# Modulation vectors by a product and a row sum on VectorE, instead of column products and matmuls on ones

## The reference

```
c_act = jax.nn.silu(c)                                 # c: (1, 1024)
for i in range(2):
    mod = c_act @ ada_w[i] + ada_b[i]                  # ada_w[i]: 1024 x 6144
    shift_t, scale_t, gate_t, shift_c, scale_c, gate_c = split(mod, 6)
    h = rmsnorm(x, norm_g[i, 0]) * (1.0 + scale_t) + shift_t
    x = x + gate_t * mixer(h)
    h = rmsnorm(x, norm_g[i, 1]) * (1.0 + scale_c) + shift_c
    x = x + gate_c * (square(relu(h @ mlp_w1[i])) @ mlp_w2[i])
```

## Time and profile before

| | us |
|---|---|
| median of 3 runs (1731.29 to 1733.81) | 1731.69 |
| the profiled execution | 1736.6 |
| its span, first to last instruction | 1735.3 |

### The profile page before, as it was taken

One profiled execution on the slowest core, in us unless ns is written; L12 is line 12 of the kernel. 1 busy time (PEld: TensorE's weight loads), 2 busy tenths in 40 slices (PEclk: granted clock), 3 DMA queues, 4 the chain that ended last, 5 costly groups with the idle time before them and its releaser, 6 DMA issues.

```text
span 1735.3 us, 18334 instructions
## 1 busy us (share of the span) xinstructions
PE 1609.7 (93%) x7266; PEld 1267.5 (73%) x7266; DVE 974.5 (56%) x1444; ACT 685.3 (39%) x1120; POOL 208.4 (12%) x194
## 2 busy tenths in 40 slices
PE   1899999799999999999998989999999899999877
PEld 1578877578888887676665768888888776777665
DVE  6665655655667564554445344343434549987544
ACT  3343432532323133444444353232323345455543
POOL 2000001100000001200000110000000103565401
PEclk9999999899999999999999989999999999999989
DMA  6534443445555533111111124333222122112111
GB/s 227 214 120 134 132 135 97 145 136 189 188 177 191 189 103 99 62 49 49 61 49 37 62 79 133 97 97 97 98 96 93 62 88 69 60 44 73 37 49 48
DMA packets 52133, 180.80 MB, mean 104 GB/s; under 512 B 5728, under 2 KB 6624, under 8 KB 51920
## 3 DMA queue, kind: packets, MB, share of 16 engines
q1 hardware_dynamic: 52048, 179.64, 31.7%
HBM read 176.08 MB, written 3.41 MB: 103 GB/s over the span
## 4 chain that ended last, share of the span: by engine, by line
PE 82%; DVE 7%; ACT 6%; POOL 2%; DMA 2%; issue 1%; SPq 0%; DVEq 0%; ACTq 0%; POOLq 0%
PE PS L424 23%; PE PS L427 22%; PE PS L425 22%; PE PS L616 2%; DVE sb_ADA L1377 2%; DVE sb_Wl L1361 1%; PE PS L438 1%; PE PS L445 1%; PE PS L627 1%; PE PS L643 1%; PE PS L740 1%; POOL sb_TMD L1970 1%; DMA sb_ARW<-ada 1%; ACT sb_Wh L896 1%; PE PS L653 1%
## 5 line engine op out<-in xcount | busy, mean ns | idle before, releaser
L424 PE MATMUL PS<-sb_Hh,sb_Wh 128*128 128x512 f32 (+2 forms) x1144 | 471.1, 412 | 21.5 <-DVE sb_Hl L1410 16.8
L427 PE MATMUL PS<-sb_Hh,sb_Wl 128*128 128x512 f32 (+2 forms) x1144 | 454.9, 398 | 0.5 <-DVE sb_Wl L1361 0.5
L425 PE MATMUL PS<-sb_Hl,sb_Wh 128*128 128x512 f32 (+2 forms) x1144 | 454.5, 397 | 0.0
L1361 DVE TENSOR_TENSOR sb_Wl<-sb_RAW,sb_Wh 128x1024 fp32r<-128x1024 f32 (+1 forms) x231 | 296.7, 1286 | 138.8 <-ACT sb_Wh L896 138.3
L896 ACT ACTIVATE sb_Wh<-sb_RAW 128x1024 fp32r<-128x1024 f32 (+1 forms) x231 | 241.8, 1048 | 248.2 <-PE PS L427 227.5
L424 PE MATMUL PS<-sb_Oh,sb_Wh 128*128 128x512 f32 x704 | 279.6, 397 | 2.8 <-DVE sb_Ol L1427 2.3
L424 PEld LDWEIGHTS PS<-sb_Hh,sb_Wh 128*128 128x128 f32 (+2 forms) x1144 | 219.7, 192 | 81.3 <-issue 30.6
L425 PE MATMUL PS<-sb_Ol,sb_Wh 128*128 128x512 f32 x704 | 276.0, 392 | 0.0
L427 PE MATMUL PS<-sb_Oh,sb_Wl 128*128 128x512 f32 x704 | 276.0, 392 | 0.0
L425 PEld LDWEIGHTS PS<-sb_Hl,sb_Wh 128*128 128x128 f32 (+2 forms) x1144 | 219.7, 192 | 50.2 <-issue 5.1
L427 PEld LDWEIGHTS PS<-sb_Hh,sb_Wl 128*128 128x128 f32 (+2 forms) x1144 | 218.9, 191 | 50.6 <-issue 1.0
(11 more groups left out here) (301 smaller groups left out, 1619.8 us busy)
## 6 DMA issues: line engine op xcount, KB each, us to landing
sb_RAW<-w SPq DMA_DIRECT2D x128, 512.0 KB, 3.5
sb_ARW<-ada SPq DMA_DIRECT2D x96, 512.0 KB, 4.5
sb_RAW<-gla_in SPq DMA_DIRECT2D x24, 512.0 KB, 3.6
sb_RAW<-diff_in SPq DMA_DIRECT2D x24, 512.0 KB, 3.5
sb_RAW<-in_b SPq DMA_DIRECT2D x16, 512.0 KB, 3.7
sb_RAW<-gla_wo SPq DMA_DIRECT2D x8, 512.0 KB, 3.6
sb_RAW<-diff_wo SPq DMA_DIRECT2D x8, 512.0 KB, 3.5
sb_RAW<-wo SPq DMA_DIRECT2D x8, 512.0 KB, 3.5
```

Of the source, the lines that this page charges most:

```text
L424: mm(to[0:m, :], Wh[:, si, k, 0:m], hi[:, k, :], start=first, stop=False)
L425: mm(to[0:m, :], Wh[:, si, k, 0:m], lo[:, k, :], start=False, stop=False)
L427: ins = mm(to[0:m, :], Wl[:, si, k, 0:m], hi[:, k, :], start=False, stop=last)
L1361: tt(Wl[:, b % 3, :, 0:m], RAW[:, b % 3, 0:8 * m].rearrange("p (k m) -> p k m", k=8), Wh[:, b % 3, :, 0:m].bitcast(F), ALU.subtract).then_ ...
```

## The change

The weights of the modulation are laid out transposed on the host: a transfer now brings 128 outputs, one on each partition, with all 1024 inputs along the row, again 512 KB. c is put on all partitions, and silu is computed there at full width, by exp, an addition, ln, exp and a product. For each transfer VectorE does one `tensor_tensor_reduce` of 128x1024: product with `CB`, row sum that begins at the bias, result in one column of `MOD`. For a scale column one small operation of one column follows. `ada_sum`, `ada_tick` and `modulation` go, with the 24 groups. Readers wait for single columns. In the start the order is by pairs of scale and shift columns for part j of h, and the weights of blocks 0, 1 and 2 are issued after transfers 3, 5 and 7. The slots of transfers 16 to 95 stay.

```diff
-ADA_GROUPS = [(0, 2), (0, 0), (0, 3), (0, 1)] + [(G // 12, G % 12) for G in range(4, 24)]
-ADA_SUM = {b + 1: s // 4 for b, s in ADA_AT.items() if s % 4 == 3}
+ADA_TILES = [(0, 8 * a + j) for j in range(8) for a in (1, 0)] + [(t // 48, t % 48) for t in range(16, 96)]
...
             def ada(s):
-                layer, g = ADA_GROUPS[s // 4]
                 if s >= 3:
-                    e.wait_ge(at("ada", s - 3, 1))
-                e.op.dma_start(ARW[:, s % 3, :], D["ada"][layer, g, s % 4]).then_inc(*landed(f"ada{s % 3}", s))
+                    e.wait_ge(at("mod", *ADA_TILES[s - 3]))
+                e.op.dma_start(ARW[:, s % 3, :], D["ada"][ADA_TILES[s]]).then_inc(*landed(f"ada{s % 3}", s))
...
             e.op.dma_start(vec[:], D["vec"]).then_inc(*landed("vec"))
+            e.op.dma_start(CB[:], D["c"].to_broadcast([P, 1024])).then_inc(*landed("c"))
...
-            for s in range(8):
+            for s in range(16):
                 ada(s)
-            weights(0)
-            weights(1)
-            for s in range(8, 16):
-                ada(s)
-            weights(2)
+                if s in (3, 5, 7):
+                    weights((s - 3) // 2)
...
-            e.wait_ge(at("ada_pe", 23))
+            e.wait_ge(at("mod", 1, 47))
...
-            def ada_sum(G):
-                to, free = TB.take(("ada", G), ("mod",) + ADA_GROUPS[G])
-                e.wait_ge(at("ada", 4 * G + 3, 1), at("one"), *free)
-                for c in range(4):
-                    ins = mm(to[:, c:c + 1], ADA[:, G % 2, c * 128:(c + 1) * 128], ones[:, 0:1], start=True, stop=True)
-                ins.then_inc(*done("ada_pe", G))
...
-            ada_sum(0)
             stat(0)
-            ada_sum(1)
-            ada_sum(2)
...
-            act(ctmp[:, 0:8], V("c", 0, 8), ACT.Exp, scale=-1.0).then_inc(*done("c_exp"))
+            cs = TMD[:].rearrange("p a t -> p (a t)")
+            e.wait_ge(at("c"))
+            act(cs, CB[:], ACT.Exp, scale=-1.0).then_inc(*done("c_exp"))
+            e.wait_ge(at("c_one"))
+            act(cs, cs, ACT.Ln).then_inc(*done("c_ln"))
+            e.wait_ge(at("c_ln"))
+            act(cs, cs, ACT.Exp, scale=-1.0).then_inc(*done("c_inv"))
...
             def ada(s):
-                G, part = s // 4, s % 4
-                acc = ADA[:, G % 2, :]
+                layer, t = ADA_TILES[s]
+                w, col = ARW[:, s % 3, :], MOD[:, layer, t:t + 1]
                 e.wait_ge(at(f"ada{s % 3}", s), at("cact"))
-                for j in range(2):
-                    k = part * 2 + j
-                    w = ARW[:, s % 3, j * T:(j + 1) * T]
-                    if k == 0:
-                        if G > 1:
-                            e.wait_ge(at("ada_pe", G - 2))
-                        ts(acc, w, cact[:, k:k + 1], None, ALU.mult).then_inc(*done("ada", s, j))
-                    else:
-                        e.wait_ge(at("ada", s, 0) if j else at("ada", s - 1, 1))
-                        stt(acc, w, cact[:, k:k + 1], acc, ALU.mult, ALU.add).then_inc(*done("ada", s, j))
+                e.op.tensor_tensor_reduce(w, w, CB[:], 1.0, V("ada_b", layer * 48 + t), ALU.mult, ALU.add,
+                                          col).then_inc(*done("mod", layer, t))
+                which, j = divmod(t, 24)
+                if 8 <= j < 16:
+                    e.wait_ge(at("mod", layer, t))
+                    stt(SC[:, layer * 2 + which, j - 8:j - 7], col, 1.0, V(f"n{layer}{which}", j - 8), ALU.add,
+                        ALU.mult).then_inc(*done("scm", layer, t))
...
-            for s in range(8):
-                ada(s)
-                if s == 4:
-                    modulation(0)
-            modulation(1)
-            w_lo(0)
-            w_lo(1)
-            for j in range(4):
-                if j:
-                    ada(7 + j)
+            for j in range(8):
+                ada(2 * j)
+                ada(2 * j + 1)
                 x_norm(0, j)
                 if j:
                     h_low(0, j - 1)
...
+                if j in (1, 2, 4):
+                    w_lo(j // 2)
             h_low(0, 7)
...
-    d["ada"] = np.ascontiguousarray(a["ada_w"].reshape(2, 4, 2, P, 12, T).transpose(0, 4, 1, 3, 2, 5)).reshape(2, 12, 4, P, 2 * T)
+    d["ada"] = np.ascontiguousarray(a["ada_w"].transpose(0, 2, 1)).reshape(2, 48, P, 1024)
+    d["c"] = np.ascontiguousarray(a["c"])
```

More of the change, by code:

```diff
@@ L268, in build @@
         bank = lambda b: PS[:, b % 2, :]
-        ada_flat = ADA[:].rearrange("p a t -> p (a t)")
-        hot = ada_flat[0:32, 0:640]
-        S2 = ada_flat[:, 0:896].rearrange("p (n v) -> p n v", v=128)
+        hot = CB[0:32, 0:640]
+        S2 = CB[:, 0:896].rearrange("p (n v) -> p n v", v=128)
         TB = Ring(sig, [PS[:, i, :] for i in (2, 3)])
@@ L275, in build @@
         TA = Ring(sig, [TMA[:, i, :] for i in range(5)])
-        TD = Ring(sig, [TMD[:, i, :] for i in range(2)])
+        TD = Ring(sig, [TMD[:, i, :] for i in range(2)], ("cact",))
         TP = Ring(sig, [TMD[:, i, :] for i in range(2)], ("c_t",))
@@ L565, in wo @@
                         add_k(b, order[n], (Oh, Ol), False, n == 7)
[L567 to L575, removed]
-                if j:
-                    ada_tick(GLA_WO + j)
+            wo(GLA_WO, 6, lambda k: at("o_lo", GLA_WO, k), lambda n: gla_tick(GLA_WO + n))
+            for j in range(2, 8):
+                project(GLA_WO + j, (Oh, Ol))
             def mlp(first, i, tick):
@@ L602, in mlp @@
                         tick(b)
-            mlp(MLP0, 1, ada_tick)
+            mlp(MLP0, 1, lambda b: None)
             stat(2)
@@ L929, in h_tile @@
                 e.wait_ge(at("xnp" if j in (2, 4, 6) else "xn", i, j),
-                          at("scm", layer, 6 * which + 2 + j // 4), at("mod", layer, 6 * which + j // 4))
+                          at("scm", layer, 24 * which + 8 + j), at("mod", layer, 24 * which + j))
                 if i:
@@ L1393, in slot @@
                     ada(ADA_AT[b])
-            def ada_tick(b):
-                if b in ADA_SUM:
-                    modulation(ADA_SUM[b])
             def x_norm(i, j):
@@ L1419, in residual @@
             def residual(first, b, j):
-                layer, g = gate_mod[first]
-                e.wait_ge(at("proj", b), at("mod", layer, g + j // 4))
+                layer, t = gate_mod[first]
+                e.wait_ge(at("proj", b), at("mod", layer, t + j))
                 stt(X[:, j, :], bank(b), gates_of[first][:, j:j + 1], X[:, j, :], ALU.mult,
@@ L1432, in one_more @@
                 ts(s, s, 1e18, 1.0, ALU.min, ALU.add).then_inc(*done("s_one", b))
+            cs = TMD[:].rearrange("p a t -> p (a t)")
             e.wait_ge(at("c_exp"))
-            ts(ctmp[:, 8:16], ctmp[:, 0:8], 1.0, None, ALU.add).then_inc(*done("c_one"))
-            e.wait_ge(at("c_one"))
-            e.op.reciprocal(ctmp[:, 0:8], ctmp[:, 8:16]).then_inc(*done("c_inv"))
-            e.wait_ge(at("c_inv"), at("vec"))
-            tt(cact[:], V("c", 0, 8), ctmp[:, 0:8], ALU.mult).then_inc(*done("cact"))
+            ts(cs, cs, 1e18, 1.0, ALU.min, ALU.add).then_inc(*done("c_one"))
+            e.wait_ge(at("c_inv"))
+            tt(CB[:], CB[:], cs, ALU.mult).then_inc(*done("cact"))
+            e.wait_ge(at("vec"))
             ts(nbr[:], V("b_r", 0, 8), -1.0, None, ALU.mult).then_inc(*done("nbr"))
@@ L1457, in dve_program @@
                     h_low(0, j - 1)
-            h_low(0, 3)
-            for s in range(11, 16):
-                ada(s)
-                if s == 12:
-                    modulation(2)
-            w_lo(2)
-            modulation(3)
-            for j in range(4, 8):
-                x_norm(0, j)
-                if j > 4:
-                    h_low(0, j - 1)
+                if j in (1, 2, 4):
+                    w_lo(j // 2)
             h_low(0, 7)
```

41 lines of the change are left out of this document (7 added, 34 removed).

## The result

The changed kernel takes 1694.62 us (median of 4 runs, 1693.87 to 1695.02) against 1732.75 us for the kernel before, run beside it (median of 4, 1731.29 to 1734.57): ratio 0.9779, 95% interval 0.9762 to 0.9796. The prediction was 1690.3, a ratio of 0.9761. The profiled execution took 1694.96 us with a span of 1693.4, 41.9 us less than the span of before; the working had 41.5.

What follows compares the result with a forecast made beforehand. TensorE was taken to bound the kernel, with 82% of the chain that ended last. 10.0 + 2.7 + 20.3 + 8.5 = 41.5 us off 1736.6 gave 1695.1, times 0.9972 gave 1690.3 us; range 1680 to 1712.

Steps and rivals of the forecast that it cites:

- The price of a tile: VectorE's new product-and-row-sum of 128x1024 takes 1.25 to 1.3 us, winning 0.2 us per tile as cover, not time.
- The sums' own cost: Each clean sum on ones costs TensorE 0.91 us: 10.0 us in the first MLP, 2.7 in the GLA stage.
- The stalls and the clock: Five sums where TensorE waits for VectorE's products: 20.3 us won, plus 8.5 us from the low clock behind them.
- what is late next: Once the stalls go, 0.6 us of TensorE waiting remains at 129 and 225 us, none at 287, 339 and 367.
- the table's forecast: Predicted change per stretch: -4.8 us to head 1's row-sum matmul, -11.7 from head 2's to the second statistics sum.
- The sum at 256 us: Fourth clean sum of the GLA stage, ahead of a wait for GpSimd's sum of squares: given no gain.
- The rest of the kernel: Stretch from the third statistics sum to the end of the span: predicted change 0.
- The start: Transfers, VectorE and ScalarE until the input's last split: 63.4 us against 63.7, counted at nothing, with -5 to +8 us.
- Half rate: Rival, chance 0.13: a tile takes 2.3 us on VectorE; start +12, GLA stage +8, MLP covered; 1710 us.
- Given back: Rival, chance 0.09: TensorE meets the next weight block or the start runs 10 us longer; 25 of 41.5 left, 1707 us.
- Slower: Rival, chance 0.06: a tile holds VectorE 3.2 us everywhere; start +24, GLA stage +21, MLP +9; 1744 us.
- Not doing what it says: Rival: a second VectorE operation per tile makes the sum, 0.2 us for reading it; no net change has chance 0.02.

Runs made afterwards that it cites:

- two_pass: The kernel after, with the fused operation split into product, sum along the row, and bias: 1721.1 us, ratio 0.9937 to the kernel before.
- idle_sums: The kernel after, with four one-column matmuls on ones at the 20 old places, waiting for nothing and read by nobody: 1713.96 us, ratio 0.9898 to the kernel before.
- con_late_after: The kernel after, with the constants' transfer and all behind it held until the sixteenth tile has landed: 1692.56 us, ratio 0.9769 to the kernel before.
- early_weights: The kernel after, with the first two weight blocks issued behind the third tile, not the fourth and sixth: 1689.25 us, ratio 0.9746 to the kernel before.
- six_ahead: early_weights, with six tiles instead of two multiplied ahead of the first normalisation: 1686.70 us, ratio 0.9727 to the kernel before.
- six_dve: early_weights, with six tiles ahead of the first normalisation and the start's normalisations all on VectorE: 1682.96 us, ratio 0.9713 to the kernel before.
- dve_norm: early_weights, with the start's three GpSimd normalisations given to VectorE: 1688.34 us, ratio 0.9742 to the kernel before.
- late_sum: The kernel before, with each group's sum on ones one block later, all 24 sums kept: 1712.25 us, ratio 0.9883 to the kernel before.

## Why the prediction was right, and where it was wrong

**The price of a tile, 1.25 to 1.3 us: right.** 1.28 us and 0.08 for the reading, and the step that chose the row of the same shape and sources over the scan's was the sound one. The half-rate rule of the Trainium skill, page "Vector Engine (DVE) Microarchitecture Reference", section "Points that are easy to get wrong", would have made it 2.3 us. For this operation the trace doesn't agree: 96 of 96 operations with two float32 sources in SBUF and an accumulator took 1.27 to 2.2 us, median 1.279, only some 50 ns more than the plain product of two_pass (1.227). The profile lists it as a custom operation; a scalar-tensor-tensor that reads its accumulator back, the form that the rule names, was run by no kernel here.

**The sums' own cost, 0.9 us: right.** In idle_sums 0.90 for each of the thirteen of the first MLP; the 0.97 of the whole run has 1.4 us in it that lie behind the last sum, in the stretch that moves by itself.

**The stalls and the clock: mechanism right, size low by about 4 us.** The step that failed is "what is late next". I took the low weight part made at 126.10 us for the next block's, and so left 0.6 us of waiting and half of the low clock at 129 and at 225. VectorE works three blocks ahead there as elsewhere; the part belonged to a later block, and the text itself says so for the three other stalls. In the kernel after nothing waits there; its timeline where TensorE goes on while VectorE makes the same low part, then a window around it:

```profile
130.91 0.60 PE L430 MATMUL PS<-sb_con,sb_TMA 128*128 128x128 f32 x4
...
131.32 1.23 DVE L1334 TENSOR_TENSOR sb_Wl<-sb_RAW,sb_Wh 128x1024 fp32r<-128x1024 f32 x1 [0.74 <-ACT sb_Wh L863]
```

```profile
125.00:135.00 10.00, 10.00 (x49) 8.33 (x48) 7.59 (x12) 5.54 (x8) 0.00 (x0) 1.00 0.41 132
```

That gives back 1.2 us of waiting and 2.4 of clock, 3.6 of the 3.8 us by which head 1 and the stretch to the second statistics sum beat the table's forecast (1.5 and 2.3). The sum at 256 us, which I gave nothing, was judged rightly: in its place stands the 1.1 us wait for GpSimd, 0.9 more than before.

**The rest of the kernel, 2.1 us: not counted.** It has no sums. The windows behind the third statistics sum differ in one place: from 30 us behind it the clock was 0.97 for 61 us before (720 to 781 us) and is 1.00 for the same work after (680 to 740), which is 1.8 of the 2.1 us. Windows of before and then of after:

```profile
720.00:781.00 61.00, 60.77 (x259) 42.82 (x258) 28.31 (x55) 22.61 (x54) 5.09 (x4) 0.97 0.16 52
```

```profile
680.00:740.00 60.00, 59.77 (x261) 41.95 (x260) 28.52 (x55) 22.92 (x55) 5.14 (x4) 1.00 0.18 54
```

It can't be put down to the change: over the twelve profiled executions of this case this stretch, the same in all, took 1043.3 to 1046.5 us, and before and after (1045.6 and 1043.5) lie inside that. What the change won behind the start is then about 46 us of the 48.1.

**The start, counted at nothing: wrong by 6.2 us, inside -5 to +8.** The steps one by one, predicted and measured: c landed at 6.98 (4 to 7); silu(c) ready at 12.2 (11); squares from 10.85 (10); additions end at 22.1 (20 to 21); the two tiles done at 18.2 (19 to 20); rstd starts at 25.95 (24.5); first split ends at 37.5 (36.4); last split ends at 69.1 (63.4). So the early chain was 1 to 1.5 us late and the step that failed is the last one, 24.7 + 2.3 us from first split to last, measured 31.7. It added up VectorE's work as if tiles were always there and each operation went at its free speed. The sixteenth tile's wait, 3.2 us, is the largest part (con_late_after: 2.6 of it is sharing with the constants and what follows them). Most of the rest is one-column work beside GpSimd, twice 0.9 us, below. The last 0.7 of the 6.2 us comes behind the last split: TensorE's clock was 0.50 there (65 to 70 us). The larger mistake is another: I found the first split waiting for weights at 33 us and put it into the sum without asking what the order cost. early_weights gives 7.0 us of last split for the moved transfers. The range's lower end, 1680, was 3 us under what its own two terms give (1690.3 - 5 - 2.4 = 1682.9).

**The rivals.** "Half rate" fell with the tile's price, and two_pass shows that its sizes for the start and the GLA stage were about fair (12 and 8 forecast, 12.3 and 8.8 found at 2.6 us) and that the MLP, put at nothing, wasn't fully covered (5.4 found). "Given back" happened in part, in the start, with 6 of the 16 us that it asked for. "Slower" had counted 3.2 us for a tile beside GpSimd; it takes 2.2 at most. "Not doing what it says": the accumulator is read by an instruction of its own, of 0.08 us.

## What to carry to other kernels

A sum on ones costs TensorE 0.23 us per column of results, what a matmul of 512 columns costs here, and a wait for another engine ahead of it costs again in the clock; on a kernel that TensorE bounds, a small reduction belongs in the engine that has the data, if an operation there does it in the same pass. Price an unseen operation by the row with its shape and its sources. Where work moves into the start, write down the order of its transfers beside the order of their readers: there the queue's order was worth 5 us, and filling VectorE's wait for rstd another 3 to 6 in the medians (six_ahead, six_dve), with intervals that overlap.

## What the runs showed of the hardware

**VectorE and GpSimd take turns, by the instruction.** I had counted doubled durations for VectorE's two-source work beside GpSimd. The start of the kernel after shows another pattern. Its timeline, then GpSimd's six additions (ns min/median/max):

```profile
12.06 10.02 POOL L1833 TENSOR_TENSOR sb_SSQ<-sb_SSQ,sb_TMA 128x512 f32<-128x512 f32 x6 [11.64 <-ACT sb_TMA L878]
...
13.63 2.20 DVE L1341 CUSTOM_DVE_ANT_0 sb_ARW<-sb_ARW,sb_CB,sb_vec 128x1024 f32<-128x1024 f32 x1
...
15.87 1.09 DVE L1346 SCALAR_TENSOR_TENSOR sb_SC<-sb_MOD,sb_vec 128x1 f32<-128x1 f32 x1
16.88 1.27 DVE L1341 CUSTOM_DVE_ANT_0 sb_ARW<-sb_ARW,sb_CB,sb_vec 128x1024 f32<-128x1024 f32 x1
...
29.27 0.16 DVE L1346 SCALAR_TENSOR_TENSOR sb_SC<-sb_MOD,sb_vec 128x1 f32<-128x1 f32 x1
```

```profile
L1833 POOL TENSOR_TENSOR sb_SSQ<-sb_SSQ,sb_TMA x6: 1261/1266/2188, 12.1 to 20.8; 128x512 f32<-128x512 f32 x6
```

The scale of one column takes 1.09 us while GpSimd adds and 0.16 when it doesn't; the tile takes 0.9 us longer or nothing. Two of GpSimd's additions (at 14.88 and 17.09) took 2.06 and 2.19 us instead of 1.26. The added time on VectorE is about 0.9 us whatever the operation's size, also in the earlier trace rows (1600 ns for 782), so it reads as the wait for the rest of one GpSimd instruction, and small operations suffer most. In the start this strikes twice more, at 44.33 (1.11 us) and 53.44 (1.09), beside GpSimd's normalisations; with these on VectorE (dve_norm) those take 0.16. It agrees with the Trainium skill, page "SBUF — State Buffer", section "Who interferes with whom": a VectorE instruction with two SBUF inputs contends with a GpSimd instruction that reads SBUF, and the one that comes first keeps the port for its whole instruction.

**A one-microsecond stop can cost three more.** In late_sum, 0.98 us of idle time and 1.39 us of one-column sums were followed by some 6 us at the lower clock. The second such pair there, 1.09 and 1.02 us at 171 us, was followed by 4 us of it. In the kernel after a wait of 1.1 us that ends at 250 us has a clock of 1.00 around it (the window 200 to 270 above), and the sums of idle_sums, with no wait beside them, leave it at 1.00 (400 to 600 us). So neither alone brought the clock down in these places; that it takes both is a reading of a few cases, and no run varied it.
